# Attention's transposes split by head group, and coefficient blocks put into free places of later rounds

## The chip, the cores and the metric

One core of one Trainium2 chip. The metric is the device time of one execution in microseconds; the kernel before has a median of 1029.72 us over three runs (1028.88 to 1030.79).

## What is computed

A decoder layer over 1024 tokens of width 1024 in float32: a state-space group and an attention group side by side, an output projection, then a mixture of experts. The change is in the attention group alone: 8 query heads over 2 key/value heads (head groups v = 0, 1, four query heads i each), with a selected branch (br 0) and a window branch (br 1, 512 tokens back). With all 16 blocks chosen the selected branch is plain causal attention. Cut to what matters:

```python
s_s = einsum('bqhgd,bhqsd->bhgqs', qc, ks) * scale + bias_s      # selected, causal
p_s = masked_softmax(s_s, dist_s >= 0)
o_s = einsum('bhgqs,bhqsd->bqhgd', p_s, vs)
s_w = einsum('bqhgd,bkhd->bhgqk', qc, kw) * scale + bias_w       # window of 512
p_w = masked_softmax(s_w, valid_w)
o_w = einsum('bhgqk,bkhd->bqhgd', p_w, vw)
o = g[..., 0:1] * o_cmp + g[..., 1:2] * o_sel + g[..., 2:3] * o_win
```

## The kernel before, in words

The stage `stage_attend` goes over 48 units. Query blocks c = 0 to 3 (128 queries each) have four units, one for each i, with both branches in a unit; c = 4 to 7 have four units of branch 0 and then four of branch 1 (window units). A unit covers both head groups. Its key blocks, 128 keys each, are its pieces, in the order head group, branch, block: 4 pieces for c = 0, 8 for c = 1, 12, 16; then 10, 12, 14, 16 for branch 0 and 10 for every window unit.

For a unit TensorE makes the scores (L1386) into banks 0 to 3. VectorE adds the bias and finds the extreme in one operation for each head group and branch (`biased`, L1443). ScalarE takes the exponential with its sum (`exps`, L1355). TensorE transposes the pieces into banks 4 and 5, at most 8 pieces in a round (L1407): each piece takes two transposes, keys 0 to 63 into one bank and 64 to 127 into the other (a "half"). Before it writes a round it waits until the round before has been copied out. The halves are copied to SBUF by `evict` (L1344), ScalarE's (index 0) and VectorE's (index 1). TensorE then multiplies values with the transposed probabilities into banks 6 and 7 (`outputs`, L1424).

The normalising factors of a query block and branch, sigmoid gate over sum, are the coefficients: VectorE computes them (`coefficients`, L1474 and L1476) after the fourth unit's exponentials, POOL widens them (L1314), TensorE transposes them as four more blocks ("w" items), and they are copied to `mix_bt`. VectorE then multiplies the four outputs of that query block by them (`mix`, L1509); only then may the next query block's outputs of that branch begin. POOL adds the product to the sum of branches (`add_branches`, L1520).

The order is fixed by the four programs, one per engine. Round plan (L1263 to L1280): a unit's pieces in order, the first 8 in round 0, the rest in round 1; the coefficient blocks of the unit before are put behind them and open a third round where they don't fit. Who copies is in `halves_of`:

```python
BOTH, ON_ACT, ON_DVE = ((0,), (1,)), ((0, 1), ()), ((), (0, 1))
halves_of += [BOTH if c < 2 else ON_DVE if n else ON_ACT for n in range(len(rounds_of[u]))]
```

So for c >= 2 ScalarE copies both halves of the first round and VectorE those of all others. TensorE's program for unit u: scores of u + 1, first round of u, outputs of u - 1, the other rounds of u. ScalarE's: first round of u, exponentials of (u + 1, v = 0), its other rounds, exponentials of (u + 1, v = 1). VectorE's: coefficients if due, `biased(u + 1, 0)`, its part of the first round, `biased(u + 1, 1)`, the other rounds, and a mix if one is due.

In the kernel before, units 4, 8, 12, 16, 32 and 40 open a query block and have a round for coefficients beyond the unit's own (in 4 it is the second, in the others the third). Unit 20, 24, 28, 36 and 44 have theirs in the second round. The last unit, 47, carries the last coefficients in its own second round.

After the stage comes the output projection (L1654), the routing and the experts (L2049 to L2128); the weights of the experts are loaded by the SP queue (L1912, L1918).

## Time and profile before

| | |
|---|---|
| median of three runs | 1029.72 us |
| the profiled execution | 1029.81 us |
| its span, first to last instruction | 1027.9 us |
| mean granted TensorE clock | 0.973 |
| TensorE busy | 959.7 us (93%) |
| VectorE busy | 494.9 us (48%) |
| ScalarE busy | 272.0 us (26%) |
| GpSimd (POOL) busy | 139.4 us (14%) |

Times are microseconds from the first instruction. PE is a matmul or transpose on TensorE, PEld a weight load for one, DVE is VectorE, ACT ScalarE, SPq the queue of DMAs. A row of a timeline merges neighbours of one kind; "x16" is their number and a bracket at the end tells how long the engine was idle before them and who ended that. Ends of matmuls are modelled, so TensorE's busy time is an upper figure. L1407 rows have two instructions for each transposed block, so x10 is five blocks. The clock is granted at 0.5 (1.2 GHz) or 1.0 (2.4 GHz).

### The profile page before, as it was taken

What the parts mean: (1) busy time and instruction counts of PE and PEld (TensorE: products, weight loads), DVE (VectorE), ACT (ScalarE), POOL (GpSimd) and SP (SyncE); (2) the same over time, 40 slices, a digit from 0 to 9 for tenths busy, and PEclk for the clock granted to TensorE, in tenths of its full rate; (3) what the DMA queues carried; (4) which work ended last, traced back from release to release, by engine and by line L of the source; (5) the groups of instructions that cost most, each with busy time, mean ns of one, the idle gap of its engine ahead of it and who ended that gap; (6) DMA issues with size and microseconds to landing.
All of it is one profiled execution on the core that took longest, in us unless ns stands there. A gap on an engine that the chain in (4) does not pass through costs nothing. (4 is left out here: it accounts for less than half of the span.)

```text
span 1027.9 us, 14602 instructions
## 1 busy us (share of the span) xinstructions
PE 959.7 (93%) x5691; PEld 568.4 (55%) x5691; DVE 494.9 (48%) x1285; ACT 272.0 (26%) x612; POOL 139.4 (14%) x136
## 2 busy tenths in 40 slices
PE   6999999999899888899998999996999997899994
PEld 4435787766555466777765455564544443444441
DVE  3496392288635377777774224276631111111126
ACT  3200111210322477677663101020101000101013
POOL 3000000131211011210011000011022221212220
PEclk9999999999999899999999999996999998999997
DMA  9310240052400190000000334657789999999966
GB/s 264 117 44 4 82 82 1 1 47 82 105 1 1 55 277 6 1 2 2 2 2 2 120 126 144 264 185 283 286 291 356 396 397 396 391 391 396 392 187 273
DMA packets 67126, 165.88 MB, mean 161 GB/s; under 512 B 38219, under 2 KB 40299, under 8 KB 54695
## 3 DMA queue, kind: packets, MB, share of 16 engines
q1 hardware_dynamic: 58928, 146.16, 39.6%
q0 software_dynamic: 7840, 18.25, 7.0%
q8 instruction: 46, 0.75, 0.3%
q10 hardware_dynamic: 288, 0.53, 0.2%
q14 instruction: 24, 0.20, 0.1%
HBM read 147.41 MB, written 25.24 MB: 168 GB/s over the span
## 5 line engine op out<-in xcount | busy, mean ns | idle before, releaser
L2058 PE MATMUL banks<-shared,wout 128*128 128x512 f32 (+1 forms) x384 | 138.9, 612 | 7.7 <-issue 6.0
L1654 PE MATMUL banks<-wout,shared 128*128 128x512 f32 x256 | 112.7, 594 | 0.5 <-PEq L1290 0.5
L2058 PEld LDWEIGHTS banks<-shared,wout 128*128 128x128 f32 (+1 forms) x384 | 53.6, 171 | 75.3 <-issue 74.8
L1355 ACT ACTIVATE shared<-shared,low 128x640 f32<-128x640 f32 (+7 forms) x128 | 93.1, 734 | 3.3 <-DVE low L1443 2.9
L386 PE MATMUL banks<-x,wout 128*128 128x512 f32 x192 | 84.6, 595 | 1.1 <-DVE x L427 1.1
L2121 DVE SCALAR_TENSOR_TENSOR mix_bt<-mix_bt,slot_coef,banks 128x256 f32<-128x256 f32 x24 | 11.5, 480 | 151.0 <-ACT mix_bt L2101 151.0
L1386 PE MATMUL banks<-shared 64*128 64x512 f32 (+3 forms) x384 | 78.9, 490 | 4.2 <-DVE low L1443 2.8
L1654 PEld LDWEIGHTS banks<-wout,shared 128*128 128x128 f32 x256 | 47.6, 190 | 55.2 <-issue 55.2
L1424 PE MATMUL banks<-shared 128*64 128x128 f32 x1056 | 69.2, 279 | 2.6 <-DVE mix_tmp L1509 1.3
L1407 PEld LDWEIGHTS banks<-consts,shared 64*128 64x128 f32 x1056 | 49.5, 140 | 31.0 <-DVE shared L1344 9.7
L2011 POOL DMA_INDIRECT x_rows<-wout,tok x22 | 35.5, 1614 | 208.8 <-DVE wout L2128 154.8
L1443 DVE CUSTOM_DVE_ANT_0 shared<-banks,bias 128x640 f32<-128x640 f32 (+4 forms) x96 | 53.2, 597 | 17.7 <-PE banks L1386 17.6
L2080 PE MATMUL banks<-shared,hidt 128*128 128x512 f32 (+1 forms) x176 | 61.6, 596 | 0.0
L1344 ACT COPY shared<-banks 128x512 f32<-128x512 f32 (+1 forms) x88 | 46.8, 579 | 55.5 <-PE banks L1407 55.5
L1424 PEld LDWEIGHTS banks<-shared 128*64 128x64 f32 x1056 | 57.4, 138 | 6.1 <-issue 1.6
L386 PEld LDWEIGHTS banks<-x,wout 128*128 128x128 f32 x192 | 35.7, 190 | 44.9 <-issue 41.9
L1407 PE MATMUL banks<-consts,shared 64*128 64x64 f32 x1056 | 57.4, 230 | 2.7 <-DVE shared L1344 1.6
L1097 PE MATMUL banks<-wout,shared 128*128 128x512 f32 x128 | 57.4, 594 | 1.5 <-PEq L738 1.5
L2101 ACT ACTIVATE mix_bt<-banks 128x256 f32<-128x256 f32 x24 | 9.2, 385 | 178.9 <-PE banks L2058 178.9
L389 PE MATMUL banks<-wout,x 128*128 128x512 f32 x128 | 55.2, 593 | 0.0
L389 PEld LDWEIGHTS banks<-wout,x 128*128 128x128 f32 x128 | 40.1, 314 | 14.6
L1344 DVE COPY shared<-banks 128x128 f32<-128x128 f32 (+3 forms) x88 | 34.6, 431 | 23.5 <-PE banks L1407 23.1
(364 smaller groups left out, 1309.3 us busy)
## 6 DMA issues: line engine op xcount, KB each, us to landing
shared<-in_exp_w_down SPq DMA_DIRECT2D x24, 1024.0 KB, 21.4
shared<-in_exp_w_gate SPq DMA_DIRECT2D x24, 1024.0 KB, 15.2
shared<-in_exp_w_up SPq DMA_DIRECT2D x24, 1024.0 KB, 21.5
x<-in_exp_w_down SPq DMA_DIRECT2D x8, 1024.0 KB, 29.5
wout<-in_w_in SPq DMA_DIRECT2D x16, 256.0 KB, 5.2
wout<-in_w_in SPq DMA_DIRECT2D x2, 2048.0 KB, 8.1
x<-in_x SPq DMA_DIRECT2D x1, 4096.0 KB, 27.8
x_rows<-x SPq DMA_DIRECT2D x8, 512.0 KB, 2.6
```

The source lines that it names most:

```text
L386: ins = nc.tensor.matmul(bank[:], slot[:, c, c0:c0 + P], ht[:, c, half * 512:half * 512 + 512], **flags)
L389: ins = nc.tensor.matmul(bank[:], tok, slot[:, c, :], **flags)
L1097: ins = nc.tensor.matmul(psum[4 + 2 * part + n % 2], wglu[:, k, c0:c0 + P], yt[:, k, (n % 2) * 512:(n % 2) * 512 + 512], start=k == 0, sto ...
L1344: ins = copy(of_half(out, h), bank[:, at:at + w])
L1355: nc.scalar.activation(prob[:, u % 2, at:at + n], prob[:, u % 2, at:at + n], ACT.Exp, bias=low[:, u % 2, v, j:j + 1], scale=-1.0, accum_ou ...
L1386: ins = nc.tensor.matmul(psum[2 * v + j][:, c0:c0 + k1 - k0], m["qt"][half, i, c * P:c * P + P], keys[half, k0:k1], start=True, stop=True)
L1407: ins = nc.tensor.transpose(half_bank(h, n), src[rows], m["ident"][rows, rows])
L1424: ins = nc.tensor.matmul(psum[6 + br][half, i * P:i * P + P], vals[:, kb, half], pt[u % 2][:, at * P:at * P + P], start=n == 0, stop=n == ...
L1443: return V.tensor_tensor_reduce(out, scores, bias, 1.0, start, ALU.add, ALU.min, least)
L1654: ins = nc.tensor.matmul(psum[n % 4], src[:, i * P:i * P + P], m["wout"][:, k, half * 512:half * 512 + 512], start=k == 0, stop=k == KD - 1)
L2058: ins = nc.tensor.matmul(psum[2 + p][rows].rearrange("p (a f) -> p a f", a=2), xt[:, p, k, rows], wgu[b][:, :, k], start=k == 0, stop=k == ...
L2080: ins = nc.tensor.matmul(psum[6 + part][rows], hidt[:, p, k, rows], wd[b][:, k, part * 512:part * 512 + 512], start=k == 0, stop=k == 1)
```

## The change

For c >= 2 the unit's pieces are split by head group: round 0 has those of v = 0, round 1 those of v = 1. Coefficient blocks no longer go with the next unit: they wait in a list, and each later unit takes as many as fit behind its round 1 (up to 8 blocks), then behind round 0 if the next query block of that branch has begun. Only blocks that are then still due open a round of their own. By this plan units 8 (2 blocks in each round, 4 in a third), 12 (a third round of 8) and 47 (a third of 4) keep an extra round; 16 takes 1 + 3 blocks, 17 three, 18 one; 20, 28 and 36 three and the unit after each one; 24 and 25 two each; 32 to 35 one each; 44 takes 1 + 3, 45 three, 46 one. Rounds fall from 94 to 92.

Copies: c = 0 goes from one half on each engine to both on VectorE; c = 1 stays; for c >= 2 round 0 is ScalarE's, round 1 VectorE's if it holds no coefficient block, and one half on each if it does; extra rounds have one half on each. The mix moves to the unit in which its last block is transposed (`mix_after`). On POOL, `add_branches` for c >= 4 comes behind the widening copy instead of before it.

```diff
@@ -1260,32 +1260,45 @@
         c, _, brs = units[u]
         return [(v, j, br, n, kb) for v in range(KV) for j, br in enumerate(brs) for n, kb in enumerate(blocks(c, br))]
-    rounds, rounds_of, of_unit, mixed_by = [], [], [], {}
+    BOTH, ON_ACT, ON_DVE = ((0,), (1,)), ((0, 1), ()), ((), (0, 1))
+    rounds, halves_of, rounds_of, of_unit, mixed_by = [], [], [], [], {}
+    last_unit = {(c, br): u for u, (c, _, brs) in enumerate(units) for br in brs}
+    first_unit = {(c, br): u for u, (c, i, brs) in enumerate(units) for br in brs if i == 0}
+    waiting = []
     for u, (c, i, brs) in enumerate(units):
         items = [("p", u, n, piece) for n, piece in enumerate(pieces(u))]
-        last = len(items)
-        for k in [u - 1] * (u > 0) + [u] * (u == len(units) - 1):
-            c0, i0, brs0 = units[k]
-            if i0 == GQA - 1:
-                for br in brs0:
-                    items += [("w", (c0, br), n, None) for n in range(4)]
-                    mixed_by[c0, br] = (len(rounds) + (len(items) - 1) // 8, k)
-        rounds_of.append(list(range(len(rounds), len(rounds) - (-len(items) // 8))))
-        of_unit.append(rounds_of[-1][:-(-last // 8)])
-        rounds += [items[n:n + 8] for n in range(0, len(items), 8)]
-    mixes = list(mixed_by)
-    BOTH, ON_ACT, ON_DVE = ((0,), (1,)), ((0, 1), ()), ((), (0, 1))
-    halves_of = []
-    for u, (c, _, _) in enumerate(units):
-        halves_of += [BOTH if c < 2 else ON_DVE if n else ON_ACT for n in range(len(rounds_of[u]))]
+        here = [items] if c < 2 else [[it for it in items if it[3][0] == v] for v in range(KV)]
+        of_unit.append(list(range(len(rounds), len(rounds) + len(here))))
+        while c >= 2 and waiting and len(here[1]) < 8:
+            here[1].append(waiting.pop(0))
+        while c >= 2 and waiting and first_unit.get((waiting[0][1][0] + 1, waiting[0][1][1]), len(units)) <= u and len(here[0]) < 8:
+            here[0].append(waiting.pop(0))
+        late = [it for it in waiting if first_unit.get((it[1][0] + 1, it[1][1]), len(units)) <= u]
+        waiting = waiting[len(late):]
+        done = [("w", (c, br), n, None) for br in brs for n in range(4)] if i == GQA - 1 else []
+        if u == len(units) - 1:
+            late, waiting = waiting + done, []
+        else:
+            waiting += done
+        at_dve = [ON_DVE] if c == 0 else [BOTH] if c == 1 else [ON_ACT, BOTH if here[1][-1][0] == "w" or late else ON_DVE]
+        halves_of += at_dve + [BOTH] * -(-len(late) // 8)
+        here += [late[n:n + 8] for n in range(0, len(late), 8)]
+        rounds_of.append(list(range(len(rounds), len(rounds) + len(here))))
+        for r, items in enumerate(here):
+            for it in items:
+                if it[0] == "w":
+                    mixed_by[it[1]] = (len(rounds) + r, u)
+        rounds += here
+    mixes = list(last_unit)
+    mixed = [[(c, br) for br in brs] if i == GQA - 1 else [] for c, i, brs in units]
+    mix_after = [[what for what in mixes if mixed_by[what][1] == u and u > last_unit[what]] for u in range(len(units))]
+    assert sum(map(len, mix_after)) == len(mixes) - 1 and not waiting
     outs = [list(itertools.accumulate(1 if h[e] else 0 for h in halves_of)) for e in range(2)]
     def evicted(eng, r):
         for e in range(2):
             if halves_of[r][e]:
                 eng.wait_ge(t_out[e], outs[e][r])
-
-    mixed = [[(c, br) for br in brs] if i == GQA - 1 else [] for c, i, brs in units]
     with nc.Block() as block:
         @block.sync
@@ -1306,13 +1319,15 @@
         @block.gpsimd
         def _(gp):
             for n, (c, br) in enumerate(mixes):
-                if c and not br:
+                if 0 < c < 4 and not br:
                     add_branches(nc, gp, m, c - 1)
                 gp.wait_ge(coef_done, n + 1)
                 if c:
                     gp.wait_ge(t_done, mixed_by[c - 1, br][0] + 1)
                 nc.gpsimd.tensor_copy(wide[:, br].rearrange("p (i v e) -> p i v e", i=GQA, v=KV),
                                       bc(mix_coef[:, br].rearrange("p (v i) -> p i v", v=KV), HD, 3)).then_inc(wide_done, 1)
+                if c >= 4 and not br:
+                    add_branches(nc, gp, m, c - 1)
         def half_bank(h, n):
             return psum[4 + h][:, n * HD:n * HD + HD]
@@ -1394,7 +1409,7 @@
                         evicted(pe, r - 1)
                     for n, (kind, whose, at, piece) in enumerate(rounds[r]):
                         if kind == "w":
-                            if at == 0 or n == 0:
+                            if n == 0 or rounds[r][n - 1][1] != whose:
                                 pe.wait_ge(wide_done, mixes.index(whose) + 1)
                             src = wide[:, whose[1], at * P:at * P + P]
                         else:
@@ -1487,12 +1502,10 @@
                     biased(u + 1, 1)
                 for r in rounds_of[u][1:]:
                     evict(dve, V.tensor_copy, r, 1)
-                if u and mixed[u - 1]:
-                    dve.wait_ge(pv_done, u)
-                    for c, br in mixed[u - 1]:
-                        r = mixed_by[c, br][0]
-                        evicted(dve, r)
-                        mix(nc, dve, m, psum, c, br)
+                for c, br in mix_after[u]:
+                    dve.wait_ge(pv_done, last_unit[c, br] + 1)
+                    evicted(dve, mixed_by[c, br][0])
+                    mix(nc, dve, m, psum, c, br)
             m["chained"] = chain.n
```

## Rows read from the trace of the kernel before

**Rows 1.** The chain that ended last, its first long piece: start us, us, what.

```profile
556.49 20.84 PE banks L1654 x48
```

**Rows 2.** The stage's stretch: busy us of PE, PEld, DVE, ACT, POOL, then clock.

```profile
354.30:557.00 202.70, 186.31 (x2626) 142.26 (x2626) 145.09 (x426) 140.40 (x346) 28.31 (x31) 0.97 0.16 44
```

**Rows 3.** Who waited for whom in the stage: us, times, longest.

```profile
PEld banks L1407 <- DVE shared L1344: 12.7, 17, 1.5
```

**Rows 4.** The stage's instructions by shape: busy us, mean ns, idle before.

```profile
L1344 ACT COPY shared<-banks 128x256 f32<-128x256 f32 x4 | 1.5, 373 | 2.8 <-PE banks L1407 2.8
...
L1344 DVE COPY shared<-banks 128x512 f32<-128x512 f32 x20 | 13.1, 686 | 5.6 <-PE banks L1407 5.6
...
L1344 DVE COPY shared<-banks 128x384 f32<-128x384 f32 x8 | 4.1, 553 | 2.8 <-PE banks L1407 2.8
...
L1344 DVE COPY shared<-banks 128x256 f32<-128x256 f32 x20 | 7.7, 419 | 4.0 <-PE banks L1407 3.9
...
L1443 DVE CUSTOM_DVE_ANT_0 shared<-banks,bias 128x640 f32<-128x640 f32 x32 | 25.1, 821 | 4.6 <-PE banks L1386 4.6
...
L1355 ACT ACTIVATE shared<-shared,low 128x640 f32<-128x640 f32 x40 | 33.0, 833 | 0.1
```

**Rows 5.** Timeline in query block 0: start us, us, instruction, idle before.

```profile
361.56 0.93 PEld L1386 LDWEIGHTS banks<-shared 64*128 64x128 f32 x8 [0.33 <-DVE low L1443]
...
363.36 0.42 DVE L1344 COPY shared<-banks 128x256 f32<-128x256 f32 x1
...
363.69 0.28 DVE L1443 CUSTOM_DVE_ANT_0 shared<-banks,bias 128x128 f32<-128x128 f32 x1
...
364.19 1.03 PEld L1386 LDWEIGHTS banks<-shared 64*128 64x128 f32 x8 [0.33 <-DVE low L1443]
```

**Rows 6.** A stretch of query block 0: engines as in rows 2, then clock.

```profile
357.30:360.70 3.40, 3.03 (x27) 2.62 (x25) 1.85 (x14) 2.05 (x11) 0.00 (x0) 0.50 1.01 402
```

**Rows 7.** Timeline of two window units of query block 6.

```profile
508.84 1.31 PE L1424 MATMUL banks<-shared 128*64 128x128 f32 x20
...
510.09 0.20 PEld L1407 LDWEIGHTS banks<-consts,shared 64*128 64x128 f32 x4 [0.17 <-ACT shared L1344]
...
511.43 0.87 PE L1407 MATMUL banks<-consts,shared 64*128 64x64 f32 x16
...
512.23 1.31 PE L1424 MATMUL banks<-shared 128*64 128x128 f32 x20
...
512.34 1.08 ACT L1344 COPY shared<-banks 128x512 f32<-128x512 f32 x2 [0.69 <-PE banks L1407]
```

**Rows 8.** Timeline where query block 4 begins (unit 16).

```profile
428.87 0.49 DVE L1344 COPY shared<-banks 128x128 f32<-128x128 f32 x2 [1.83 <-PE banks L1407]
...
430.47 0.20 PEld L1407 LDWEIGHTS banks<-consts,mix_wide 64*128 64x128 f32 x4 [1.78 <-DVE mix_bt L1344]
...
430.65 1.30 PE L1386 MATMUL banks<-shared 64*128 64x128 f32 x8
...
431.26 1.28 DVE L1509 TENSOR_TENSOR mix_tmp<-banks,mix_bt 128x512 f32<-128x512 f32 x2
...
432.37 1.31 PE L1424 MATMUL banks<-shared 128*64 128x128 f32 x20
```

**Rows 9.** Timeline: third rounds of units 8, 12, 32, 40; the last outputs.

```profile
388.86 0.33 PEld L1407 LDWEIGHTS banks<-consts,mix_wide 64*128 64x128 f32 x8 [1.66 <-DVE mix_bt L1344]
...
408.43 0.57 PEld L1407 LDWEIGHTS banks<-consts,mix_wide 64*128 64x128 f32 x16 [1.52 <-DVE shared L1344]
...
490.04 0.20 PEld L1407 LDWEIGHTS banks<-consts,mix_wide 64*128 64x128 f32 x4 [1.65 <-DVE mix_bt L1344]
...
523.91 0.32 PEld L1407 LDWEIGHTS banks<-consts,mix_wide 64*128 64x128 f32 x8 [1.52 <-DVE shared L1344]
...
554.70 1.07 PEld L1424 LDWEIGHTS banks<-shared 128*64 128x64 f32 x20 [1.39 <-DVE mix_bt L1344]
```

**Rows 10.** Timeline of the DMA queue: the first expert weights.

```profile
576.28 0.42 SPq L1918 DMA_DIRECT2D shared<-in_exp_w_down  x1
```

## The prediction

> **What bounds the kernel now.** I read the chain that ended last first. From 556.49 us on it is TensorE alone, beginning with the output projection [rows 1]; the reader is to see that nothing of the long tail began before the attention stage handed TensorE over. The first expert weights are issued at 576.28 [rows 10], after that hand-over, and each later load is released by a step of the projection or of an expert, so no transfer of the tail runs on a schedule of its own. A microsecond taken off the attention stage should therefore move everything behind it by the same amount. Then I read the stage's own stretch: 202.70 us, TensorE busy for 186.31, VectorE 145.09, ScalarE 140.40 [rows 2]. No engine is full, TensorE is nearest, and its busy time hides waits, because ends are modelled. The waits name the gap: weight loads of transposes waited 12.7 us for VectorE's copies out of banks 4 and 5, in 17 stalls of up to 1.5 us [rows 3]. The timelines show where, and there the sum is made.
>
> **A steady unit.** Query blocks 4 to 7 have 20 window or 640-column global units. One takes 512.23 - 508.84 = 3.39 us [rows 7]. TensorE goes round outputs, second round, scores, first round. In it: the second round waits 0.17 us for ScalarE's two copies; the first round holds 0.80 us (511.43 to 512.23), because three of its eight blocks are of the second head group and need that group's exponentials; and ScalarE stands idle 0.69 us until that round is done [rows 7]. Loads of transposes cost 0.20 for 4, 0.33 for 8 and 0.57 for 16 [rows 9], so about 0.38 for 10. After the change both rounds have five blocks, ten loads. The first round then costs 0.38 plus some 0.06 of hand-over instead of 0.80 (-0.36); the second 0.38 instead of 0.20 (+0.18); the 0.17 goes, as ScalarE's two copies shrink from 512 columns, 1.08 together [rows 7], to 320, some 0.76 (one of 256 takes 373 ns [rows 4]). Period 3.39 - 0.36 + 0.18 - 0.17 = 3.04.
>
> What is late next? VectorE gets the longer copies. A copy of 320 columns lies between 419 and 553 ns [rows 4], say 0.49; the next operation starts about 0.09 before the first has ended (363.36 to 363.69 for one of 0.42 [rows 5]), so two take 0.89. From the second round's start to the next first round that makes 0.57 (round and hand-over, as the 0.38 plus what rows 8 show between a round and its copy) + 0.89 + 0.05 = 1.51, against TensorE's own way of 0.36 + 1.17 for scores = 1.53 (1.17 is 511.43 - 510.09 less 0.17 for the short round [rows 7]). It just fits; I take 3.08. VectorE's whole work is 2 x 0.82 + 0.89 = 2.53 and ScalarE's 2 x 0.83 + 0.76 = 2.42 [rows 4], both under 3.08.
>
> Few units have this in full, since the coefficient blocks taken off elsewhere come back here at 0.03 per load. By place: one clean interval -0.3; four with one coefficient block, three of them with a VectorE product of 0.64 (two take 1.28 [rows 8]), -0.2 each; two with three blocks, -0.1 each; six in front of units with 768 or more columns, whose longer scores hide the first round's wait already, -0.13 each. Together **-2.1**. Units of query block 2 (three, -0.2) and the global ones of 5 (three, -0.13): **-1.0**. Units of query block 3, of 6 global and 7 global, already have seven or eight blocks in each round: 0.
>
> **Third rounds that vanish (units 16, 32, 40).** Unit 16 in full [rows 8]. Its second round ends just ahead of VectorE's first copy at 428.87; the third round waits 1.78, until 430.47; scores start at 430.65, the products run 431.26 to 432.54 and the outputs start at 432.37. After: the second round ends at the same time, ScalarE and VectorE take a half each, 320 + 192 columns: 0.49 for the first and some 0.3 more for the second (two of 128 columns take 0.49 [rows 8], one of 256 takes 0.42), 0.75 us in all, to 429.6; ScalarE, a little quicker, 0.65. Scores start at 428.7 and last 1.17; the first round goes 429.84 to 430.28; one product is done by 430.35; outputs at 430.4 instead of 432.37, -1.97. Units 32 and 40 stalled 1.65 and 1.52 [rows 9], and their rounds' 0.12 to 0.3 goes too: -1.8 each. Together **-5.6**.
>
> **Third rounds that stay (8, 12; 4 is unchanged).** They stalled 1.66 and 1.52 [rows 9] on VectorE copying both halves. In unit 12 the second round's copies go from two of 0.69 [rows 4] in a row to one on each engine; ScalarE reaches its own 0.25 late, behind exponentials: -0.43. The coefficients' four copies of 256 columns become two on each engine: -0.67. So -1.1; unit 8, with smaller rounds, -0.8. **-1.9**.
>
> **Coefficients in a second round (20, 24, 28, 36, 44).** VectorE alone copied two blocks or four of each half and the coefficients behind them (0.49 and two of 256 columns, 0.75, in the narrow case: 1.24) where scores cover 1.17; now each engine takes 0.75 and the product moves a unit on: -0.2 to -0.4 each, **-1.6**. In unit 44 the outputs now wait for a product that had long been done; it ends within 0.1 of when they are due, and I count that in.
>
> **The end.** The last outputs waited 1.39 for VectorE [rows 9]. The second round there becomes five blocks shared by both engines, the one before needs one group's exponentials only, and a third round of four blocks comes ahead of the outputs, +0.3: **-0.8**.
>
> **Query block 0 loses.** Its four units go from one half on each engine to both on VectorE, which stands in the loop scores, reduction, copy, reduction, scores: scores wait 0.33 for VectorE in each unit [rows 5]. A second copy of 256 columns adds 0.33 (363.36 to 363.69). Four units: **+1.3**. On this the Trainium skill (VectorE: DVE Perf Modes, Rules for kernel authors) says to keep the number of VectorE operations small, since the next one starts only when the last has drained; read as no overlap at all, the loss would be 4 x 0.42 = 1.7 and the sum 1018.5. The row shows an overlap of 0.09, and the sum goes by the row.
>
> **POOL** adds branches after the widening copy from block 4 on, instead of before it; the sums wait for products, and wide copies were never the last thing waited for there: 0. The range for this is 0 to +0.5. The DMAs are untouched.
>
> **Sum.** -2.1 - 1.0 - 5.6 - 1.9 - 1.6 - 0.8 + 1.3 = -11.7. Against the profiled execution's 1029.81 (the median of the runs is 1029.72, the same within 0.01%) that is **1018.1 us**.
>
> **Rivals.**
> The first: VectorE's longer copy takes the place of ScalarE's wait. The two ways above, 1.51 and 1.53, differ by less than I can read. If copy, semaphore and a product behind it come 0.3 late, steady units stay at 3.39, and the terms -2.1, -1.0 and -1.6 go: 1029.8 - 7.0 = 1022.8. For it: the 17 stalls of rows 3 are of this kind. Against: VectorE has 0.5 us free per unit. 17%.
>
> The second, slower: ScalarE's queue. In 18 units with coefficients it must now copy the second round between its two exponentials. If it stands bare there 0.69, as it does today before the first round [rows 7], and again before the first round, a window unit takes 2 x 0.83 + 0.76 + 0.65 + 1.38 = 4.45 where I have 3.2: 18 x 1.25 = +22.5, so 1040.6. It decides from 11.7 / 18 = 0.65 us per such unit. Against: the second wait is just what the split removes. 5%. With a single such wait, +0.57 x 18 = +10.3, 1028.4, which is no change or nearly; with the next one, 4%.
>
> The third: the change doesn't reach the end, because the expert stage, which moves the most data, takes the time back in waits for weights: 1029.8. Against it, rows 10 and the order of the loads. It is in the 4%.
>
> The fourth: the clock. In query block 0 TensorE was granted 0.50, its 1.2 GHz level, while it was busy 3.03 of 3.40 us [rows 6], after waiting at the stage's start, and full speed came afterwards. Slower units there could keep it low for one more such stretch, which costs at most half of it, 1.7: 1019.8. The Trainium skill (TensorE: Matmul & The Clock Gate, HAM oscillation) has gaps in TensorE's work bring the clock down; here only query block 0 gets wider gaps, and every other place gets narrower ones. 6%.
>
> **Chances.** Forecast 68%, with a range of its own of 1015.5 to 1020.5 (every term moved by a quarter); the rivals 17, 5, 4 and 6%. The range of 8 in 10, 1014.5 to 1023.5, takes in the first and the fourth. Below 0.2%, 2 us, a measurement of this kernel can tell nothing from no change; so faster 0.91, same 0.04, slower 0.05.
>
> **What would show it.** Stage stretch near 191 us instead of 202.7. Window units without coefficients 3.05 to 3.15 us from outputs to outputs; ScalarE's 0.69 before its copies gone. No transposes of coefficients in a round of their own at units 16, 32 and 40, and 4.1 to 4.3 us between their outputs. VectorE's copies of 320 columns near 0.49 us. Query block 0 at 2.96 us per unit instead of 2.63 (361.56 to 364.19). After the hand-over the same lengths as before to within 2 us. Wrong would be: steady units still at 3.39; ScalarE idle ahead of its copies of second rounds; or a tail that is longer by what the stage saved.

## The result, and the profile after it

The changed kernel takes 1021.38 us (median of 4 runs, 1020.94 to 1022.24) against 1030.26 (4 runs, 1028.88 to 1031.07) before: ratio 0.9918, 95% interval 0.9905 to 0.9931. It is faster by 8.9 us, where 11.7 was forecast. The profiled execution took 1021.36 us with a span of 1019.5 us, against 1029.81 and 1027.9.

The chain that ended last, its first long piece (start us, us, what), which answers to [rows 1]:

```profile
549.72 20.84 PE banks L1667 x48
```

The attention stage's stretch (length, then busy us of PE, PEld, DVE, ACT, POOL, clock, DMA share, GB/s), which answers to [rows 2]:

```profile
357.30:549.80 192.50, 182.24 (x2625) 140.02 (x2625) 142.69 (x400) 146.58 (x392) 27.81 (x31) 0.98 0.17 47
```

From the first scores to the projection the stage went from 202.15 us (354.34 to 556.49) to 192.38 (357.34 to 549.72): -9.8. The part behind it (the tail) took 469.8 us against 471.4. Ahead of it 3.0 us more passed, in code that the change doesn't touch; in the twelve kernels below the stage began at 354.7 to 357.2, and the tail took 468.8 to 474.9 (short_product's aside, which can't be compared). So head and tail scatter by some microseconds, and **the stage's length is what the experiments are read by**. Because its first units see the low clock of [rows 6] at different moments, I also give its length from the outputs of unit 5 on ("behind unit 5"): 179.44 before, 169.50 after. This length repeats closely: c0_both below, whose code is the changed kernel's from unit 4 on, has 169.53. Each experiment was run once unless runs are counted beside it.

Waits in the stage (who waited for whom: us, times, longest), which answer to [rows 3]:

```profile
PEld banks L1422 <- ACT mix_bt L1359: 10.4, 20, 1.2
...
PEld banks L1422 <- issue: 9.5, 50, 0.3
PEld banks L1422 <- DVE shared L1359: 8.8, 14, 1.1
```

The 12.7 us in which transposes waited for VectorE's copies of probabilities are 8.8 now, and 10.4 stand against ScalarE's copies of coefficient blocks. Before the change a second row, which the prediction does not name, stood against VectorE's copies of coefficient blocks:

```profile
PEld banks L1407 <- DVE mix_bt L1344: 10.7, 10, 1.8
```

With the smaller rows (4.1 and 0.2 us for ScalarE's copies before, 2.6 after) the waits for copies were 27.7 us and are 21.8. The wait did not go; it was shortened and spread over two engines. The copies by shape, which answer to [rows 4]:

```profile
L1359 ACT COPY shared<-banks 128x320 f32<-128x320 f32 x53 | 20.6, 428 | 14.6 <-PE banks L1422 14.2
...
L1359 DVE COPY shared<-banks 128x320 f32<-128x320 f32 x27 | 12.6, 489 | 10.9 <-PE banks L1422 10.6
L1359 DVE COPY shared<-banks 128x512 f32<-128x512 f32 x19 | 12.5, 687 | 5.1 <-PE banks L1422 5.0
...
L1359 ACT COPY shared<-banks 128x512 f32<-128x512 f32 x21 | 11.5, 588 | 11.7 <-PE banks L1422 11.7
```

VectorE's copy of 320 columns, taken at 0.49 us, measures 0.489.

**Where the 9.8 us came from**, by intervals (interval or "unit" u runs from the outputs of unit u - 1 to those of unit u, as the 3.39 us of [rows 7] for unit 37; after less before):

| term | forecast | measured |
|---|---|---|
| steady units of blocks 4 to 7 | -2.1 | -0.1 |
| block 2 and global units of block 5 | -1.0 | 0.0 |
| third rounds gone (16, 32, 40) | -5.6 | -5.5 (-1.71, -1.91, -1.84) |
| third rounds that stay (8, 12) | -1.9 | -1.7 (-0.70, -0.99) |
| coefficients in a second round (20, 24, 28, 36, 44) | -1.6 | -1.7 (-0.39, -0.53, -0.41, -0.40, +0.07) |
| the end (46, 47) | -0.8 | -0.4 |
| query block 0 (0 to 3) | +1.3 | +0.2 |
| units forecast at nothing (4, 13 to 15, 33 to 35, 41 to 43) | 0 | -0.6 |
| sum | -11.7 | -9.8 |

Unit 16 beside [rows 8], timeline (start us, us, instruction, idle before):

```profile
429.69 1.30 PE L1401 MATMUL banks<-shared 64*128 64x128 f32 x8
429.90 0.43 ACT L1359 COPY shared<-banks 128x320 f32<-128x320 f32 x1 [0.74 <-PE banks L1422]
429.90 0.49 DVE L1359 COPY shared<-banks 128x320 f32<-128x320 f32 x1 [1.70 <-PE banks L1422]
430.22 0.32 ACT L1359 COPY mix_bt<-banks 128x192 f32<-128x192 f32 x1
430.31 0.35 DVE L1359 COPY mix_bt<-banks 128x192 f32<-128x192 f32 x1
...
430.83 0.47 PE L1422 MATMUL banks<-consts,shared 64*128 64x64 f32 x10
430.85 0.69 DVE L1522 TENSOR_TENSOR mix_tmp<-banks,mix_bt 128x512 f32<-128x512 f32 x1 [0.20 <-DVE mix_bt L1359]
...
431.69 0.55 PE L1439 MATMUL banks<-shared 128*64 128x128 f32 x6 [0.39 <-DVE mix_tmp L1522]
```

Both engines copy at the same time and are done at 430.66 (0.76 us after they began; forecast 0.75), and the scores cover it. The wait of 1.78 is gone. The outputs wait 0.39 for the product, which ends 0.3 us behind the first round where I had the two end together; so the unit gained 1.71 and not 1.97.

And a steady unit with one coefficient block, beside [rows 7]:

```profile
504.45 1.31 PE L1439 MATMUL banks<-shared 128*64 128x128 f32 x20
...
505.70 0.39 PEld L1422 LDWEIGHTS banks<-consts,shared 64*128 64x128 f32 x10 [0.17 <-issue]
...
506.12 1.30 PE L1401 MATMUL banks<-shared 64*128 64x128 f32 x8
...
507.26 0.47 PE L1422 MATMUL banks<-consts,shared 64*128 64x64 f32 x10
...
507.66 1.31 PE L1439 MATMUL banks<-shared 128*64 128x128 f32 x20
```

The first round costs 0.40 us (507.26 to 507.66) instead of 0.80, as forecast. But the 0.17 in front of the second round is still there, now with no engine named: ScalarE's two copies of 0.75 us had begun at 504.57 and ended at 505.32, 0.38 ahead of it. The period is 3.21.

### The profile page after: what moved, and what is told of

Same layout as the page of the kernel before. It is cut to its first block and busy times, and to the rows that moved or that the text cites. A ratio compares the mean times of both kernels' runs of the same rounds, so it can differ in the third digit from the quotient of the medians.

```text
span 1019.5 us, 14663 instructions
## 1 busy us (share of the span) xinstructions
PE 957.4 (94%) x5691; PEld 567.2 (56%) x5691; DVE 493.3 (48%) x1259; ACT 278.2 (27%) x658; POOL 139.3 (14%) x136
## 5 line engine op out<-in xcount | busy, mean ns | idle before, releaser
L1359 ACT COPY shared<-banks 128x320 f32<-128x320 f32 (+3 forms) x105 | 46.5, 482 | 34.0 <-PE banks L1422 33.1
L1359 DVE COPY shared<-banks 128x320 f32<-128x320 f32 (+4 forms) x71 | 37.4, 553 | 21.9 <-PE banks L1422 21.5
```

Source lines behind the costliest of these rows:

```text
L1359: ins = copy(of_half(out, h), bank[:, at:at + w])
```

## The experiments

My theory after these traces: the split by head group is worth next to nothing, and the gain is that of **sharing copies** between two engines and of **spreading coefficient blocks** over later units. The rival, from the prediction: the split takes a wait out of every steady unit, and what hides it is a new wait (VectorE's longer copies, or its products).

### One engine or two in query block 0; sharing every second round; a short product

c0_both gives query block 0 its half on each engine back; all_shared lets both engines copy every second round; short_product multiplies only 64 of the 512 columns of a product. The rest of the mix is left out there, what the expert stage is given differs from then on, and only the stage's own stretch can be compared.

```diff
# c0_both
-        at_dve = [ON_DVE] if c == 0 else [BOTH] if c == 1 else [...]
+        at_dve = [BOTH] if c < 2 else [...]
# all_shared
-        ... else [ON_ACT, BOTH if here[1][-1][0] == "w" or late else ON_DVE]
+        ... else [ON_ACT, BOTH]
# short_product, in mix
-    nc.vector.tensor_tensor(m["mix_tmp"][:, br], psum[6 + br], m["mix_bt"][:, br], ALU.mult)
+    nc.vector.tensor_tensor(m["mix_tmp"][:, br, 0:64], psum[6 + br][:, 0:64], m["mix_bt"][:, br, 0:64], ALU.mult)
```

> Query block 0 copies one half on each engine again, the rest as in the changed kernel. If the single VectorE copy in the loop of scores and reductions is what that block pays for, units 1 to 3 go from 2.92, 3.21 and 3.56 us back to about 2.64, 2.66 and 3.6 and the stage is 0.6 to 1.3 us shorter than the changed kernel's (192.4). If the first units are set by TensorE's low clock instead, they stay within 0.2.

Measured: 1021.15 us, stage 192.43 (192.38 in the changed kernel); the 0.6 to 1.3 us did not come. Units 1 and 2 did come back, to 2.63 and 2.42 us, but unit 3 took 4.05 and unit 0 6.37 instead of 5.79: units 0 to 3 take 15.48 us in both, against 15.28 before. They lie in and behind the low-clock stretch of [rows 6], which is not equally long in all kernels. With one half on each engine they took 15.28, 15.48, 14.40 and 14.86 us in four kernels (before, c0_both, split_alone, before_shared; mean 15.0), with both on VectorE and the coefficients where they were 15.2 to 16.2 in seven (mean 15.7). Kernels in which the clock was granted at 0.5 for an equally long time can be set side by side:

| granted 0.5 for | one half on each engine | both on VectorE |
|---|---|---|
| 10.2 to 10.3 us | 15.28 (before), 15.48 (c0_both) | 15.87 (late_product) |
| 6.8 us | 14.86 (before_shared) | 15.48 (the change), 15.70 (all_shared), 15.54 (unshared) |
| 3.4 us | 14.40 (split_alone) | 15.20 (short_product) |

So the term is some +0.5 to +0.8 (all from single runs that scatter by some tenths), and not +1.3. The measured pair shows less, +0.2, and the two ran at the low clock for different times, the kernel before from 354.6 to 364.8 and the changed one from 361.8 to 368.6. Unit 1 takes 2.6 to 2.9 us with VectorE alone, 2.5 to 2.6 otherwise; in the changed kernel 2.92, its outputs being:

```profile
363.13 1.12 PE L1439 MATMUL banks<-shared 128*64 128x128 f32 x8
366.05 1.12 PE L1439 MATMUL banks<-shared 128*64 128x128 f32 x8
```

> From query block 2 on every second round is copied half by half, so VectorE no longer takes two copies of 320 columns (0.89 us) alone. Theory A (VectorE's longer copy holds up the units after a product): the units of 3.66 to 3.72 us fall to 3.2 to 3.3, the stage is 3 to 4 us shorter. Theory B (the product of 0.69 us, moved into steady units, holds them up): they fall by the share of VectorE's time that is freed, to about 3.4, the stage is 1 to 2 us shorter. Rival to both: ScalarE, which must now copy between its exponentials in every unit, takes it back, and the stage is longer.

Measured: 1019.99 us, stage 191.81, behind unit 5 168.72 (-0.8). Intervals 14, 42 and 43, with 512 columns in each copy, lose 0.47 us each, and 22 and 26 lose 0.18; 11, 15 and 23 take 0.41, 0.29 and 0.27 more. Units 19, 30 and 38 stay at 3.67, 3.73 and 3.94, so neither theory A nor theory B came as stated, and ScalarE did not take it all back either. So sharing is worth something where the prediction had none (two copies of 512 columns on VectorE), and costs something where a unit also makes coefficients.

> The product of outputs and coefficients covers 64 of its 512 columns only (the other columns of the attention output are left out), about 0.2 us instead of 0.69, all else as in the changed kernel. Theory B (product): the units that follow one (19, 22, 30, 38) fall from 3.66 to 3.94 us to 3.2 to 3.5 and the stage is 2 us shorter or more. Theory A (copy): they stay above 3.6, and the stage is shorter by no more than 1 us, at units 8 and 12 where outputs wait for products.

Measured: stage 190.14, behind unit 5 168.23 (the whole time, 1193.63 us, says nothing here). Units 16 and 44 lose 0.46 and 0.47, units 4 and 5 some 0.35 each, 8 and 12 0.16 and 0.24: there the product is the last thing waited for. Units 30 and 38, right behind a product, lose 0.16 each, of which 31 and 39 take back as much. Unit 22, whose predecessor carries a product too, stays at 3.69, and 19 goes from 3.66 only to 3.63. So the product does delay some of the units that follow it (the rival), but it is not what holds 19 and 22, and most of the 2.2 us came elsewhere than theory B had them.

### Without spreading; coefficients later; products later; spreading without the split

```diff
# no_spread
-        while c >= 2 and waiting and first_unit.get(...) <= u and len(here[0]) < 8:
+        while c >= 2 and waiting and len(here[0]) < 8:
-        late = [it for it in waiting if first_unit.get(...) <= u]
+        late = list(waiting)
# spread_only
-        here = [items] if c < 2 else [[it for it in items if it[3][0] == v] for v in range(KV)]
+        here = [items] if c < 2 else [items[0:8], items[8:]]
# late_product
+    mix_at = {what: mixed_by[what][1] + (what in ((3, 1), (4, 0), (4, 1), (5, 0), (5, 1), (6, 0))) for what in mixes}
-    mix_after = [[what for what in mixes if mixed_by[what][1] == u and u > last_unit[what]] for u in range(len(units))]
+    mix_after = [[what for what in mixes if mix_at[what] == u and u > last_unit[what]] for u in range(len(units))]
# coef_later, on VectorE
-                if mixed[u]:
-                    coefficients(u)
                 if u + 1 < len(units):
                     biased(u + 1, 0)
...
                 if u + 1 < len(units):
                     biased(u + 1, 1)
+                if mixed[u]:
+                    coefficients(u)
```

> Pieces split by head group as changed, but all coefficient blocks go with the next unit again, as far as its two rounds have places, the rest in a third round; so do the products. The spreading's part: units 32 and 40 get a third round back (2 and 4 blocks), +1.5 to +1.8 us each, unit 16 one of 2 blocks, +1.5. Theory B: the units after products (19, 22, 30, 38) get their 0.3 us back each, so the sum is +3.5 us or so on the stage. If the split alone had made the change, the stage would be unchanged within 1 us.

Measured: 1025.82 us, stage 197.41. Units 16, 32 and 40 have their third rounds again, at 5.21, 5.23 and 5.50 us against 4.44, 3.88 and 4.16; 21, 29 and 37, whose second round then holds no coefficient block and is VectorE's alone, take 3.44 instead of 3.21. Units 19, 22, 30 and 38 lose 0.40, 0.34, 0.16 and 0.16. Spreading is worth 5.0 us of the stage on top of the rest, 4.3 behind unit 5.

> The changed kernel with VectorE's coefficients behind both score reductions of the next unit instead of ahead of them. Theory C (in unit 19 and before the units with more columns, VectorE stands at the coefficients until ScalarE's last exponentials, so the next scores come late): interval 19 goes from 3.66 to about 3.3 us, 31 and 39 fall by 0.1 to 0.3, 23 by 0.1, the stage is 1 to 2 us shorter. Theory B (product alone): no interval moves by over 0.1.

Measured: 1017.83 us, stage 191.13. Behind unit 5 it is 167.93 (-1.6). Unit 19 loses 0.36, as theory C had it, but 23, 31 and 39 do not move. Most of the gain is where I had not looked: unit 7 goes from 4.83 to 3.83, a wait that the kernel before had as well, and 11 loses 0.26. Unit 22 keeps its 3.69. The row of the changed kernel shows what unit 7 lost: scores behind the reductions that stand behind two coefficient computations.

```profile
386.58 0.62 PEld L1401 LDWEIGHTS banks<-shared 64*128 64x128 f32 x5 [1.26 <-DVE low L1458]
```

> The changed kernel with six of the products moved one unit on, into units whose second round has no coefficient block (or the next one's). Theory B (product delays the two reductions behind it by 0.35 us, then the second head group's scores start late): intervals 22, 30 and 38 fall by 0.1 to 0.3 and the next ones rise by as much, unless VectorE has a gap there; the stage stays within 1 us. Theory C: 19 stays at 3.66 or falls by no more than 0.1.

Measured: 1021.06 us, stage 193.26. Unit 22 loses 0.34 and 30 and 38 lose 0.16, but 23 takes 0.54 more, and 31, 36 and 39 take 0.26, 0.17 and 0.16 more: nothing is gained in sum (169.98 behind unit 5, against 169.50). The product does make the next unit late when VectorE alone copies behind it, but moved it makes another late. Unit 22 in the changed kernel shows how:

```profile
447.92 0.69 DVE L1522 TENSOR_TENSOR mix_tmp<-banks,mix_bt 128x512 f32<-128x512 f32 x1 [0.20 <-DVE mix_bt L1359]
...
448.70 0.82 DVE L1458 CUSTOM_DVE_ANT_0 shared<-banks,bias 128x640 f32<-128x640 f32 x1
...
449.45 0.82 DVE L1458 CUSTOM_DVE_ANT_0 shared<-banks,bias 128x640 f32<-128x640 f32 x1
...
450.03 1.85 PE L1401 MATMUL banks<-shared 64*128 64x256 f32 x8
...
450.24 0.89 DVE L1359 COPY shared<-banks 128x320 f32<-128x320 f32 x2
...
451.38 0.81 PE L1422 MATMUL banks<-consts,shared 64*128 64x64 f32 x10
...
452.12 1.31 PE L1439 MATMUL banks<-shared 128*64 128x128 f32 x20
```

These two reductions follow the product directly, and the second one ends at 450.27, behind the start of the next scores (450.03). These take 1.85 us, where scores of the same shape take 1.51 in late_product's unit 22, since the second head group's half of them has to wait for its bank. The first round behind them takes 0.74 (451.38 to 452.12) instead of 0.40, ten loads in each case. In late_product the unit takes 3.35.

The product is not the only thing that holds these reductions. In short_product it ends 0.5 us sooner, and the first reduction still begins 0.27 us behind the start of the outputs (446.50 there), as in the changed kernel:

```profile
445.99 0.23 DVE L1522 TENSOR_TENSOR mix_tmp<-banks,mix_bt 128x64 f32<-128x64 f32 x1 [0.20 <-DVE mix_bt L1359]
446.77 0.82 DVE L1458 CUSTOM_DVE_ANT_0 shared<-banks,bias 128x640 f32<-128x640 f32 x1 [0.55 <-PE banks L1422]
```

The same reduction of units 30 and 38 begins 0.09 ahead of the outputs with the short product and 0.10 behind them with the whole one, and those units lose their 0.16. In late_product, where no product stands there, unit 22's begins 0.10 ahead (446.12 against 446.22). What VectorE waited for at 446.22 in short_product is not shown: the profile names TensorE's transposes, but the program asks there only for those of unit 21, the last of which ended at 445.13.

> The first eight pieces in the first round again, as before the change, with coefficient blocks spread over later units, shared copies and moved products as changed. If the split by head group brings next to nothing in steady units (as the comparison without spreading suggests: 3.28 and 3.20 against 3.39), the stage is within 1 us of the changed kernel's 192.4, and it is the spreading and sharing that made the gain. If the split brings what the prediction gave it (terms of -2.1 and -1.0), it is 2.5 to 3.5 us longer.

Measured: 1026.76 us (with a tail of 474.9 us, the longest of all), stage 194.70, behind unit 5 170.94. The stage is 2.3 us longer than the changed kernel's, outside both ranges; but 0.9 of that lies in the first units, and behind unit 5 it is 1.4. So without the split the changed kernel would have kept 8.5 of its 9.9 us behind unit 5 (179.44 to 169.50). Units 18, 21, 29 and 37, which have before's split here and no coefficient block, take 3.19 to 3.20 us; the changed kernel's take 3.20 to 3.21 with one block, whose two loads cost some 0.06 by the prediction's price. A steady unit is within 0.1 us the same with either split. What the split gives lies in units with two or three coefficient blocks (20, 24, 28 and 36 take 0.28 to 0.30 less with it), and 19, 22, 26, 27, 30 and 38 give 0.14 to 0.34 back.

### The split alone, sharing alone, all but sharing

So far the spreading and the split have been taken out. Now the split and the sharing are each tried alone, and then the sharing is taken out.

```diff
# split_alone: no_spread's two edits, and
-        at_dve = [ON_DVE] if c == 0 else [BOTH] if c == 1 else [ON_ACT, BOTH if ... else ON_DVE]
-        halves_of += at_dve + [BOTH] * -(-len(late) // 8)
+        at_dve = [BOTH] if c < 2 else [ON_ACT, ON_DVE]
+        halves_of += at_dve + [BOTH if c < 2 else ON_DVE] * -(-len(late) // 8)
# before_shared, in the kernel before
-        halves_of += [BOTH if c < 2 else ON_DVE if n else ON_ACT for n in range(len(rounds_of[u]))]
+        halves_of += [BOTH if c < 2 or n else ON_ACT for n in range(len(rounds_of[u]))]
# unshared, in the changed kernel
-        at_dve = [...] if c == 1 else [ON_ACT, BOTH if here[1][-1][0] == "w" or late else ON_DVE]
-        halves_of += at_dve + [BOTH] * -(-len(late) // 8)
+        at_dve = [...] if c == 1 else [ON_ACT, ON_DVE]
+        halves_of += at_dve + [BOTH if c < 2 else ON_DVE] * -(-len(late) // 8)
```

> The changed kernel's split by head group with before's order of the rest: no piece is brought forward, a second round holds the second head group's pieces and those of coefficient blocks that are due, third rounds stay, and VectorE alone copies every round from the second on, as before. My theory by the runs so far, that the split is worth nothing in a steady unit: the stage (first scores to first projection) takes 200 to 204 us against 202.15 in the kernel before, units 18, 21, 29 and 37 take 3.15 to 3.4 us, and units 16, 32 and 40 keep their third rounds at 5.3 to 5.8 us. The prediction's theory, that the split takes a wait out of every steady unit: the stage takes 198 to 199 us, 0.15 us less in each of some 20 units.

Measured: 1027.97 us, stage 202.50, against 202.15 before. Units 18, 21, 29 and 37 take 3.20, 3.40, 3.38 and 3.39 us, before 3.19, 3.39, 3.39 and 3.39. The prediction's 3 us for the split are not there. Units 16, 32 and 40 keep their third rounds at 5.83, 5.84 and 6.01 us, against 6.15, 5.79 and 6.00 before.

> The kernel before with one edit: every round of transposes from a unit's second on is copied half by ScalarE and half by VectorE; rounds, split and order are before's. If sharing a copy is worth by itself what it was worth on top of the change: units 14, 42 and 43 lose 0.4 to 0.5 us each, units 16, 32 and 40 with their third rounds lose 0.3 to 0.6 each, and the stage takes 198 to 200 us against 202.15. If the gain needs the fuller second rounds, and ScalarE's exponentials are the next to be late: these units lose under 0.2 us and units with six pieces in the second round (17 to 39) gain nothing or take 0.1 to 0.3 longer, with the stage at 202 to 204 us.

Measured: 1025.29 us, stage 196.92. **One line in the kernel before is worth 5.2 us of the stage**, 4.8 behind unit 5. Units 14 and 42 lose 0.47 each, 43 only 0.19; 8 and 12 lose 0.82 and 0.99, no less than in the changed kernel; 16, 32 and 40 lose 0.68, 0.61 and 0.49 with their third rounds still there. Units 11 and 15 take 0.25 and 0.36 more, as with all_shared: there ScalarE's part of the copy stands ahead of exponentials that the coefficients wait for. Units 18 and 46, with two pieces in the second round, take 0.17 and 0.18 more. The stage is 1 us under the range that I gave. The third round of unit 8, with 1.16 us of waiting where [rows 9] had 1.66:

```profile
387.57 0.42 DVE L1344 COPY shared<-banks 128x256 f32<-128x256 f32 x1 [0.89 <-PE banks L1407]
387.85 0.37 ACT L1344 COPY shared<-banks 128x256 f32<-128x256 f32 x1
387.91 0.41 DVE L1344 COPY mix_bt<-banks 128x256 f32<-128x256 f32 x1
388.10 0.39 ACT L1344 COPY mix_bt<-banks 128x256 f32<-128x256 f32 x1
388.55 0.32 PEld L1407 LDWEIGHTS banks<-consts,mix_wide 64*128 64x128 f32 x8 [1.16 <-ACT mix_bt L1344]
```

> The changed kernel with its rounds as they are (split by head group, coefficient blocks spread) but with before's rule for the copies: VectorE alone copies every round behind the first. So far: split alone 202.50 us of stage, split and shared copies without spreading 197.41, all of the change 192.38, sharing on the kernel before 196.92. If spreading and sharing are worth the same each, wherever they are put (about 5 us and 5 us): the stage takes 196.5 to 198.5 us. If spreading needs the shared copies, because a second round of eight blocks is more than VectorE can copy while the scores run (1.37 us for two copies of 512 columns): the units whose second round is filled (17, 20, 25, 28, 33, 36) take 0.3 to 0.6 us more than in the changed kernel, 16, 32 and 40 lose only 1.0 to 1.4 us of their third rounds instead of 1.7 to 1.9, and the stage takes 199 to 201 us.

Measured: 1032.08 us, stage 202.81, above both ranges. Units 16, 32 and 40 do lose their third rounds (-1.15, -1.73, -1.84), and it all goes back: units that carry a coefficient block take 3.53 us where the changed kernel's take 3.21 (18, 21, 29, 37), 17 and 45 take 3.93 instead of 3.33, 34 and 35 0.6 and 0.5 more. The timeline of unit 37 there, beside the steady unit above:

```profile
512.75 1.30 PE L1401 MATMUL banks<-shared 64*128 64x128 f32 x8
512.96 0.89 DVE L1359 COPY shared<-banks 128x320 f32<-128x320 f32 x2 [0.90 <-PE banks L1422]
...
513.76 0.35 DVE L1359 COPY mix_bt<-banks 128x64 f32<-128x64 f32 x2
514.16 0.39 PEld L1422 LDWEIGHTS banks<-consts,shared 64*128 64x128 f32 x10 [0.94 <-DVE mix_bt L1359]
514.16 0.53 PE L1422 MATMUL banks<-consts,shared 64*128 64x64 f32 x10
514.20 0.69 DVE L1522 TENSOR_TENSOR mix_tmp<-banks,mix_bt 128x512 f32<-128x512 f32 x1
```

VectorE copies for 1.15 us (512.96 to 514.11) where scores cover 1.14 (506.12 to 507.26 in the changed kernel's unit 37), and with the hand-over on either side of the copies the first round is 0.27 us later behind the scores' start than it was (514.16 - 512.75 = 1.41 against 1.14). This is the prediction's first rival, in a kernel that does not share.

The four kernels with the split, behind unit 5, and the three without:

| behind unit 5, us | nothing spread | spread |
|---|---|---|
| split, VectorE copies alone | 180.67 (split_alone) | 179.86 (unshared) |
| split, rounds with coefficients shared | 173.78 (no_spread) | 169.50 (the change) |
| before's split, VectorE alone | 179.44 (before) | |
| before's split, shared | 174.62 (before_shared: every second and third round) | 170.94 (spread_only: rounds with coefficients) |

On top of the split, sharing alone is worth 6.9 us, spreading alone 0.8, both together 11.2: 3.5 us belong to neither. Without the split sharing every later round is worth 4.8; spreading without the split and without sharing was not run. The split costs 1.2 alone and gives 1.4 on top of the two.

### A version that beats both

> Second rounds copied half by half, coefficients behind the reductions and products one unit later, all at once. If VectorE's row of work is what keeps steady units over TensorE's own 3.2 us (theories A, B and C together), clean window units reach 3.2 to 3.3 and the stage is 3 to 5 us shorter than the changed kernel's 192.4: 1016.5 to 1018.5 us. If ScalarE, which is full in units with shared rounds, takes over as the bound, the stage is within 1 us of the changed kernel's.

all_three is all_shared, coef_later and late_product together. Measured: 1016.70 us (4 runs, 1013.3 to 1018.4), ratio to before 0.9865 (0.9841 to 0.9889), stage 187.53.

> The changed kernel with two edits together: every second round is copied by both engines, half each, and the coefficients of a product unit stand behind both bias reductions on VectorE instead of ahead of them. The products stay where the changed kernel has them. If the two gains add (0.6 and 1.25 us of the stage when each was tried alone): the stage takes 190.3 to 190.8 us and the time is 1.5 to 2.5 us under the changed kernel's. If each removes what the other left (with copies shared VectorE is free early enough for the coefficients, wherever they stand, but the coefficients wait for the later exponentials): the stage takes 187.5 to 189.5, near the kernel that had the later product too (187.53), and the later product is worth nothing here either, as when it was tried alone.

all_shared and coef_later alone. Measured: 1016.26 us (4 runs, 1015.89 to 1017.62), ratio 0.9863 (0.9839 to 0.9888), stage 187.50. The later products are worth nothing here either. The two edits that gave 0.6 and 1.25 us of the stage one at a time give 4.9 together (behind unit 5, where the low clock plays no part: 0.8 and 1.6 one at a time, 4.2 together). Units 11 and 15, which lost 0.41 and 0.29 when only the copies were shared, gain 0.44 and 0.47 now. In all_shared VectorE stood at the coefficients, waiting for exponentials that the shared copy had made later, and the reductions behind them began 0.66 us behind the outputs that open interval 11 (400.85 against 400.19); in the changed kernel it was 0.25 (402.04 against 401.79). With the coefficients behind the reductions that wait is gone. The stage's stretch:

```profile
355.50:543.10 187.60, 179.73 (x2625) 140.47 (x2625) 132.88 (x381) 154.71 (x411) 27.70 (x31) 0.98 0.17 48
```

VectorE has 9.8 us less to do than in the changed kernel and ScalarE 8.1 more. This version's interval ends below that of the change (0.9888 against 0.9905), though the two were run on different chips, each beside the kernel before.

## Why the prediction was right, and where it was not

**The path to the end** was right. The projection follows at 549.72 as it did at 556.49, with the same first piece of 20.84 us, and the tail was 1.6 us shorter than before, not longer by what the stage had saved.

**Third rounds and coefficients in second rounds**, 9.1 of the 11.7 us, were right within 0.3 us in sum (-8.8). Most of these were read from stalls with a row of their own, and the replacement was priced from copies in the same trace. Unit 44 had the wrong sign (+0.07): its outputs wait for a product, which had been put at 0.1, and which is worth 0.47 there by short_product.

**The steady unit** failed, and with it 3.1 us: "Period 3.39 - 0.36 + 0.18 - 0.17 = 3.04". There were two errors in it. The 3.39 us of [rows 7] are not a steady unit's but that of a unit right behind one with a product. Its two reductions stood behind that product and began with the outputs:

```profile
508.24 0.69 DVE L1509 TENSOR_TENSOR mix_tmp<-banks,mix_bt 128x512 f32<-128x512 f32 x1
508.84 0.81 DVE L1443 CUSTOM_DVE_ANT_0 shared<-banks,bias 128x640 f32<-128x640 f32 x1
```

In spread_only, where unit 36's copies are shared, the same product begins at 503.86, the reductions 0.31 us ahead of the outputs (504.47 against 504.78), and unit 37 takes 3.19 us. Unit 18 of the kernel before is such a cleaner one, and I had not looked for it:

```profile
435.84 1.31 PE L1424 MATMUL banks<-shared 128*64 128x128 f32 x20
...
437.09 0.20 PEld L1407 LDWEIGHTS banks<-consts,shared 64*128 64x128 f32 x4 [0.17 <-ACT shared L1344]
...
437.26 1.30 PE L1386 MATMUL banks<-shared 64*128 64x128 f32 x8
...
438.40 0.70 PE L1407 MATMUL banks<-consts,shared 64*128 64x64 f32 x16
...
439.03 0.33 PE L1424 MATMUL banks<-shared 128*64 128x128 f32 x2
```

It takes 3.19 us: 1.25 with the gap, 0.17, 1.14 and 0.63. The changed kernel's takes 1.25, 0.42, 1.14 and 0.40, of which 0.06 is for the two loads of the coefficient block that it carries. The twenty loads have to be paid in whichever rounds they are put; the split saves some 0.04 us where the copies are in time. And the 0.17 was not ScalarE's: from unit 9 on it is there wherever transposes follow outputs, in all fourteen kernels (but for gaps of 0.29 at units 24 and 32 in no_spread and split_alone), whether the copies were done 0.4 us before or just in time. The releaser named beside it was only the last semaphore to have come.

**The first rival**, at 17%, came half. Six of the units whose second round VectorE alone copies (19, 22, 26, 27, 30, 38) became 0.14 to 0.34 us longer than before, though 11 and 23 became 0.27 and 0.31 shorter. In spread_only, with before's split, 22, 26, 27, 30 and 38 are as long as before; sharing takes 0.18 from 22 and 26, a later product 0.34 from 22 and 0.16 from 30 and 38, and later coefficients 0.36 from 19. So in most of them it is the longer copy together with what stands ahead of it on VectorE; none of these edits alone moved 27. Its price was right for the terms -2.1 and -1.0, which are gone, though mostly since there was nothing to win. It was wrong for the coefficients' -1.6, which came in full, because those rounds are shared. Its time, 1022.8, is nearer to the result than the forecast, for a reason that it did not give.

**Query block 0**: +0.2 in the measured pair, with a shorter low-clock stretch as luck, and some +0.5 to +0.8 where that stretch is equally long, instead of +1.3. The overlap in the price held: two copies of 320 columns take 0.89 us where one takes 0.49, so 0.09 overlap again. The Trainium skill (VectorE: DVE Perf Modes, The DRAIN you can't avoid) has the next operation start only when the pipeline of the last is empty, and adds that one which is not held starts earlier. The rows here agree with the addition, and the prediction had cited the page without it. **The end** gave 0.4 of 0.8: the third round of four blocks waits 0.74 us for ScalarE's copy, where 0.3 had been put for the whole of it.

```profile
547.51 0.35 PEld L1422 LDWEIGHTS banks<-consts,mix_wide 64*128 64x128 f32 x8 [0.74 <-ACT shared L1359]
```

**What was put at nothing** (units of block 3, global ones of 6 and 7) gave 0.6, and 14, 42 and 43 had another 0.47 each to give: two copies of 512 columns on one engine, 1.29 us, do not fit beside scores of 1.14 (the scores in these intervals are already those of a 640-column unit). That sum stood in the prediction for the coefficient units and had not been made for these.

ScalarE's queue, the clock and the tail, the other rivals, did not come: ScalarE stood idle 0.17 us ahead of its copy of a second round (unit 21, where the rival had 0.69) and not at all ahead of the next first round's, and the stage's low-clock stretch was 6.8 us where it had been 10.2.

So the prices of the third rounds and of the coefficients were right, and the mechanism that the split was given was wrong. The stage's sum is off by 1.9 of 11.7 us, and that is in part luck. The steady units and those of block 2 and global 5 alone put it off by 3.0, and the end by 0.4; query block 0 (1.1 better than forecast) and the units put at nothing (0.6) went the other way.

## What to carry to other kernels

Before a gain is multiplied by the number of "steady" units, find the shortest unit of that kind in the trace: if one already runs at the length that the change is to bring, the rest wait for something else. Where one engine's copies have to fit beside another's work, add them up for every width, also where the change leaves them alone, and try to give each engine half first: here that one line was worth half of the gain, and spreading the work without it next to nothing (0.8 us). Two edits that each remove part of a wait can be worth far more together than their sum, when each alone leaves an engine standing in front of the other's work.

## What the runs showed that I had not expected

- TensorE leaves 0.17 us between a run of outputs (128x64 loads) and the first transposes (64x128 loads) behind them, whatever the copies do; the kernel before and all changed ones have it from unit 9 on.
- The same ten loads of a first round take 0.40 us when the scores ahead of them end together, and 0.74 when the second head group's scores began late; the scores themselves, for 768 columns, go from 1.51 to 1.85 us.
- No 640-column unit with another's scores beside it took less than 3.14 us (unit 19 in all_three). TensorE counts as busy for 95% of the changed kernel's stage (182.24 of 192.50 us), and that stage could still lose 4.9 us.
- With code that does not differ, the part behind the stage took 468.8 to 474.9 us, and the part ahead of it 354.3 to 357.3. Single times of kernels that differ by 2 us say nothing. The stage's own length does: unit 37 took 3.20 or 3.21 us in all eight kernels in which it has one block and a shared copy.
